# Three-branch attention of one layer: the compressed branch of two heads through one block-diagonal product

## The reference, cut to what matters

```python
k_cmp = compress(kvh(kc), pe_k, w1_k, w2_k)      # 31 compressed keys per key/value head
v_cmp = compress(kvh(vc), pe_v, w1_v, w2_v)
s = jnp.einsum('bsgrd,bngd->bgrsn', q, k_cmp).astype(jnp.float32) * scale
p, denom, _ = masked_softmax(s + bias_c, dist_c >= 0)
p_cmp = p / jnp.maximum(denom, 1e-30)
o_cmp = jnp.einsum('bgrsn,bngd->bsgrd', p_cmp, v_cmp.astype(jnp.float32))
...
o = g[..., 0:1] * o_cmp + g[..., 1:2] * o_sel + g[..., 2:3] * o_win
```

## Time and profile before

| what | us |
|---|---|
| median of the runs | 2892.97 |
| the profiled execution, its own time | 2896.67 |
| span of its trace, first to last instruction | 2894.5 |
| attention stage in it, first score product to the last drain | 1607.7 to 1761.5 |
| distance from one pair's drain to the next in the steady part | 18.56 |
| PE busy in the span | 2708.1 (94%) |
| DVE busy | 1883.1 (65%) |
| ACT busy | 843.7 (29%) |
| POOL busy | 1185.5 (41%) |

### The profile page before, as it was taken

One profiled execution on the slowest core, in us unless ns is written; L12 is line 12 of the kernel. 1 busy time (PEld: TensorE's weight loads), 2 busy tenths in 40 slices (PEclk: granted clock), 3 DMA queues, 4 the chain that ended last, 5 costly groups with the idle time before them and its releaser, 6 DMA issues.

```text
span 2894.5 us, 35802 instructions
## 1 busy us (share of the span) xinstructions
PE 2708.1 (94%) x12080; PEld 1729.9 (60%) x12080; DVE 1883.1 (65%) x4890; ACT 843.7 (29%) x1653; POOL 1185.5 (41%) x837
## 2 busy tenths in 40 slices
PE   8998999999877877799999999999999999999999
PEld 3364454444333332244447777888888877788887
DVE  8988788888888888777765786544223336554411
ACT  4732111111111111121123785322232127522222
POOL 5314444444444444344440233444434434444443
PEclk9999999999999999999999999999999999999999
DMA  4169999999999999999996221222322222122232
GB/s 131 62 238 372 417 412 421 421 418 420 412 421 419 414 422 414 421 421 420 420 420 229 64 69 53 96 99 94 107 87 99 93 67 67 66 95 95 102 101 79
DMA packets 130308, 700.38 MB, mean 242 GB/s; under 512 B 16694, under 2 KB 28886, under 8 KB 64343
## 3 DMA queue, kind: packets, MB, share of 16 engines
q0 software_dynamic: 74352, 543.04, 45.6%
q1 hardware_dynamic: 54760, 153.30, 15.7%
q10 hardware_dynamic: 1072, 2.41, 0.2%
HBM read 696.41 MB, written 2.28 MB: 241 GB/s over the span
## 4 chain that ended last, share of the span: by engine, by line
PE 49%; DMA 19%; issue 14%; DVE 8%; POOL 7%; ACT 3%; POOLq 0%; DVEq 0%; SPq 0%; ACTq 0%
DMA arena<-in_peer_uv,arena 18%; PE ps L543 16%; PE ps L883 14%; POOL w_lo L420 6%; PE ps L2363 4%; DVE arena L1216 3%; PE ps L911 2%; ACT arena L1662 1%; PE ps L2021 1%; PE ps L1570 1%; DVE arena L1227 1%; PE ps L795 1%; PE ps L1556 1%; PE ps L1542 1%; PE ps L773 1%
## 5 line engine op out<-in xcount | busy, mean ns | idle before, releaser
L883 PE MATMUL ps<-arena 128*128 128x512 f32 x2048 | 954.7, 610 | 145.6 <-DVE arena L1227 144.6
L1350 POOL DMA_INDIRECT arena<-in_peer_uv,arena x512 | 570.0, 1113 | 785.0 <-PE ps L883 723.4
L883 PEld LDWEIGHTS ps<-arena 128*128 128x128 f32 x2048 | 382.7, 193 | 653.7 <-issue 383.6
L1216 DVE CUSTOM_DVE_ANT_0 arena<-arena,sq 128x1024 f32<-128x1024 f32 x512 | 607.4, 1224 | 194.3 <-DMA arena<-in_peer_uv,arena 190.7
L420 POOL TENSOR_TENSOR w_lo<-ring,w_hi 128x1024 fp32r<-128x1024 f32 (+1 forms) x156 | 407.4, 2612 | 514.8 <-ACT w_hi L433 514.8
L543 PE MATMUL ps<-n_hi,w_hi 128*128 128x512 f32 x992 | 387.6, 391 | 0.5 <-issue 0.3
L543 PE MATMUL ps<-n_hi,w_lo 128*128 128x512 f32 x992 | 386.1, 389 | 0.0
L543 PE MATMUL ps<-n_lo,w_hi 128*128 128x512 f32 x992 | 382.0, 389 | 0.2 <-DVE n_lo L470 0.2
L1043 ACT ACTIVATE dots_gel<-dots_gel,tok_scale 128x2 f32<-128x2 f32 x256 | 75.7, 296 | 1002.2 <-DVE dots_gel L1216 1002.0
L433 ACT CAST w_hi<-ring 128x1024 fp32r<-128x1024 f32 (+1 forms) x156 | 174.6, 1120 | 644.3 <-PE ps L543 644.3
L543 PEld LDWEIGHTS ps<-n_hi,w_hi 128*128 128x128 f32 x992 | 186.2, 188 | 40.9 <-issue 2.4
(11 more groups left out here) (364 smaller groups left out, 3619.4 us busy)
## 6 DMA issues: line engine op xcount, KB each, us to landing
ring<-in_a_up SPq DMA_DIRECT2D x44, 512.0 KB, 3.5
ring<-in_b_up SPq DMA_DIRECT2D x44, 512.0 KB, 3.5
ring<-in_a_in SPq DMA_DIRECT2D x40, 512.0 KB, 7.7
ring<-in_b_q SPq DMA_DIRECT2D x24, 512.0 KB, 3.5
ring<-in_a_down SPq DMA_DIRECT2D x16, 704.0 KB, 4.0
ring<-in_b_down SPq DMA_DIRECT2D x16, 704.0 KB, 4.0
ring<-in_w_in SPq DMA_DIRECT2D x16, 512.0 KB, 3.5
arena<-in_peer_uv,arena POOLq DMA_INDIRECT x512, 10.9
```

The source lines that it names most:

```text
L883: mm = pe.matmul(bank(2 * (tt % 2) + q), diag[:, no % DIAGS, r, :], uvrow[p][r][:, D + 512 * q:D + 512 * q + 512], start=slot + r == 0, st ...
L1216: ins = dve.tensor_tensor_reduce(out=u, in0=u, in1=ntok[:, tt, :], scale=1.0, scalar=0.0, op0=ALU.mult, op1=ALU.add, accum_out=dots[:, p, ...
L1350: pool.indirect_dma_start(uvrow[p][r], None, t["peer_uv"], bass.IndirectOffsetOnAxis(ap=expert_id[:, tt, slot + r:slot + r + 1], axis=0)). ...
```

## The change

The compressed keys of the two halves are kept as a block-diagonal matrix (half 0 in rows 0 to 63 and columns 0 to 30, half 1 in rows 64 to 127 and columns 32 to 62, zeros elsewhere), and so are the compressed values (rows 0 to 30 with columns 0 to 63, rows 32 to 62 with columns 64 to 127). The scores of the compressed branch of both halves are then one product over all 128 rows with 63 columns, into bank 1 beside win 0; both blocks of probabilities are one transpose of 63 columns; and the output of both halves is one product over 63 rows with 128 output rows. Around it: the order of the products is sel 0, sel 1, cmp, win 0, win 1; DVE scales both compressed branches in one instruction and POOL only win 1; the last chunk of transposes is one block shorter; the row maxima of half 1 come as sel, cmp, win. ACT copies keys and values with four instructions instead of two, and DVE clears the padding.

```diff
-        kcmp = a.take(2, NCMP)
-        vcmp = a.take(256)
+        kcmp = a.take(2, 2, CMP_PAD)
+        vcmp = a.take(2, 2, DH)
...
+        def both_compressed(s):
+
+            it, qt = divmod(s, TT)
+            return (ps[:, 1, 384:384 + CMP_BOTH], proj[:, it, P * qt:P * qt + P],
+                    kcmp[:, it // GR].rearrange("p a b -> p (a b)")[:, 0:CMP_BOTH],
+                    vcmp[0:CMP_BOTH, it // GR].rearrange("p a b -> p (a b)"))
...
-        PE_ORDER = (("sel", 0), ("sel", 1), ("win", 0), ("win", 1), ("cmp", 0), ("cmp", 1))
-        DVE_ORDER = (("sel", 0), ("win", 0), ("cmp", 0), ("sel", 1), ("win", 1), ("cmp", 1))
-        READS_BEFORE = (1, 4, 3, 6, 3, 6)
-        SCORES_BEFORE = (1, 5, 5, 2, 6, 6)
+        PE_ORDER = (("sel", 0), ("sel", 1), ("cmp", None), ("win", 0), ("win", 1))
+        DVE_ORDER = (("sel", 0), ("win", 0), ("cmp", 0), ("sel", 1), ("cmp", 1), ("win", 1))
+        READS_BEFORE = (1, 4, 5, 5, 6)
+        SCORES_BEFORE = (1, 4, 4, 2, 4, 5)
...
-            return full + [(half, sides[half]["cmp"].blocks[0]) for half in range(2)], len(full)
+            return full + [(1, (Both.at, Both.width, both_compressed(s)[3]))], len(full)
...
-                    pe.matmul(b.scores, b.q, b.keys, start=True, stop=True).then_inc(LA.scores_ready, 1)
+                    if name == "cmp":
+                        to, q, keys, _ = both_compressed(s)
+                    else:
+                        b = branches(s, half)[name]
+                        to, q, keys = b.scores, b.q, b.keys
+                    pe.matmul(to, q, keys, start=True, stop=True).then_inc(LA.scores_ready, 1)
...
-                mm.then_inc(LA.pv_done, 1)
+                x, (_, width, v) = len(order) - 1, order[-1][1]
+                pe.matmul(ps[:, OUT_BANK, P * qt:P * qt + P], v, ptA[0:width, s % 2, P * x:P * x + P],
+                          start=False, stop=True).then_inc(LA.pv_done, 1)
...
-                for b in sides[0].values():
+                for b in (sides[0]["sel"], sides[0]["win"]):
...
-                dve.tensor_scalar(pr, pr, invA[:, s % 3, 1, 1:2], None, ALU.mult).then_inc(LA.scaled, 1)
-
+                dve.tensor_scalar(pr, pr, invA[:, s % 3, 1, 1:2], None, ALU.mult)
+                pr = pA[:, s % 3, Both.at:Both.at + 2 * CMP_PAD].rearrange("p (a b) -> p a b", a=2)[:, :, 0:NCMP]
+                dve.tensor_tensor(pr, pr, invA[:, s % 3, :, 0:1].broadcast_to([P, 2, NCMP]), ALU.mult).then_inc(LA.scaled, 1)
...
-                for b in (side["win"], side["cmp"]):
-                    pr = pA[:, s % 3, b.at:b.at + b.width]
-                    ins = pool.tensor_scalar(pr, pr, invA[:, s % 3, 1, b.slot:b.slot + 1], None, ALU.mult)
-                ins.then_inc(LA.scaled_rest, 1)
+                b = branches(s, 1)["win"]
+                pr = pA[:, s % 3, b.at:b.at + b.width]
+                pool.tensor_scalar(pr, pr, invA[:, s % 3, 1, b.slot:b.slot + 1], None, ALU.mult).then_inc(LA.scaled_rest, 1)
...
-            act.copy(kcmp, ps[:, 4, 0:62]).then_inc(cmp_copied, 1)
-            act.copy(vcmp[0:NCMP, :], ps[0:NCMP, 5, 0:256]).then_inc(cmp_copied, 1)
+            keep_keys()
+            keep_values()
...
+            dve.memset(kcmp, 0.0)
+            dve.memset(vcmp, 0.0)
```

More of the change, by code:

```diff
@@ L49 @@
 CMP_POS = 32
+CMP_PAD = 32
+CMP_BOTH = CMP_PAD + NCMP
 NEG = -1e30
@@ L1486, in branches @@
             wide = keys - P * k0
-            q, base = proj[rows, it, cols], 928 * half
+            q, base = proj[rows, it, cols], 896 * half
             return {
@@ L1492, in branches @@
                               tabA[:, it % 2, half, 896 - wide:896], 2, [vtok[:, 1, x, kv] for x in range(k0, qt + 1)]),
-                "cmp": Branch(half, 2 * half + 1, 384, NCMP, base + 896, q, kcmp[rows, gp, :],
-                              tcmp[:, heads(it)[half], 24 - 8 * qt:24 - 8 * qt + NCMP], 0, [vcmp[0:NCMP, kv]])}
-        PE_ORDER = (("sel", 0), ("sel", 1), ("win", 0), ("win", 1), ("cmp", 0), ("cmp", 1))
-        DVE_ORDER = (("sel", 0), ("win", 0), ("cmp", 0), ("sel", 1), ("win", 1), ("cmp", 1))
-        READS_BEFORE = (1, 4, 3, 6, 3, 6)
-        SCORES_BEFORE = (1, 5, 5, 2, 6, 6)
+                "cmp": Branch(half, 1, 384 + CMP_PAD * half, NCMP, 1792 + CMP_PAD * half, None, None,
+                              tcmp[:, heads(it)[half], 24 - 8 * qt:24 - 8 * qt + NCMP], 0, [None])}
+        def both_compressed(s):
[3 more added lines that the diff above has]
+                    vcmp[0:CMP_BOTH, it // GR].rearrange("p a b -> p (a b)"))
+        class Both:
+            at, width = 1792, CMP_BOTH
+        PE_ORDER = (("sel", 0), ("sel", 1), ("cmp", None), ("win", 0), ("win", 1))
+        DVE_ORDER = (("sel", 0), ("win", 0), ("cmp", 0), ("sel", 1), ("cmp", 1), ("win", 1))
+        READS_BEFORE = (1, 4, 5, 5, 6)
+        SCORES_BEFORE = (1, 4, 4, 2, 4, 5)
+        PER_SCORES = len(PE_ORDER)
         def turn_list(s):
@@ L1565, in values @@
                 order, _ = turn_list(s)
-                sides = [[(x, b) for x, (half, b) in enumerate(order) if half == side] for side in range(2)]
+                sides = [[(x, b) for x, (half, b) in enumerate(order[:-1]) if half == side] for side in range(2)]
                 for y in range(len(sides[0])):
@@ L1569, in values @@
                         x, (_, width, v) = sides[half][y]
-                        mm = pe.matmul(ps[64 * half:64 * half + 64, OUT_BANK, P * qt:P * qt + P], v,
-                                       ptA[0:width, s % 2, P * x:P * x + P], start=y == 0, stop=y == len(sides[0]) - 1)
-                mm.then_inc(LA.pv_done, 1)
+                        pe.matmul(ps[64 * half:64 * half + 64, OUT_BANK, P * qt:P * qt + P], v,
+                                  ptA[0:width, s % 2, P * x:P * x + P], start=y == 0, stop=False)
+                x, (_, width, v) = len(order) - 1, order[-1][1]
+                pe.matmul(ps[:, OUT_BANK, P * qt:P * qt + P], v, ptA[0:width, s % 2, P * x:P * x + P],
+                          start=False, stop=True).then_inc(LA.pv_done, 1)
             scores(0)
@@ L1609, in row_max @@
                     b = branches(s, half)[name]
-                    dve.wait_ge(LA.scores_ready, PER * s + SCORES_BEFORE[x])
+                    dve.wait_ge(LA.scores_ready, PER_SCORES * s + SCORES_BEFORE[x])
                     dve.tensor_tensor_reduce(
@@ L1641, in scale @@
                 pr = pA[:, s % 3, b.at:b.at + b.width]
-                dve.tensor_scalar(pr, pr, invA[:, s % 3, 1, 1:2], None, ALU.mult).then_inc(LA.scaled, 1)
+                dve.tensor_scalar(pr, pr, invA[:, s % 3, 1, 1:2], None, ALU.mult)
+                pr = pA[:, s % 3, Both.at:Both.at + 2 * CMP_PAD].rearrange("p (a b) -> p a b", a=2)[:, :, 0:NCMP]
+                dve.tensor_tensor(pr, pr, invA[:, s % 3, :, 0:1].broadcast_to([P, 2, NCMP]), ALU.mult).then_inc(LA.scaled, 1)
+            dve.wait_ge(hc_ready, 4)
+            for x in range(3):
+                dve.memset(pA[:, x, Both.at + NCMP:Both.at + CMP_PAD], 0.0)
             for s in range(STEPS + 2):
@@ L1659, in exponentials @@
                     act.wait_ge(LA.bank_read, PER * s + 3 * half + 3)
-                    for b in branches(s, half).values():
+                    for b in (branches(s, half)[x] for x in ("sel", "cmp", "win")):
                         pr = pA[:, s % 3, b.at:b.at + b.width]
@@ L2055, in layer_a_pe @@
                 u, half = divmod(g, 2)
+                rows = slice(CMP_PAD * half, CMP_PAD * half + NCMP)
                 for tile in range(2):
-                    mm = pe.matmul(ps[0:NCMP, 5, 64 * g:64 * g + 64], hg[:, 1, tile, half, NCMP * u:NCMP * u + NCMP],
+                    mm = pe.matmul(ps[rows, 5, 64 * g:64 * g + 64], hg[:, 1, tile, half, NCMP * u:NCMP * u + NCMP],
                                    w2[:, 1, tile, :], start=tile == 0, stop=tile == 1)
@@ L2069, in layer_a_act, with keep_keys, keep_values @@
         def layer_a_act(act):
+            def keep_keys():
+                for half in range(2):
+                    rows = slice(64 * half, 64 * half + 64)
+                    ins = act.copy(kcmp[rows, :, half, 0:NCMP], ps[rows, 4, 0:2 * NCMP].rearrange("p (a b) -> p a b", a=2))
+                ins.then_inc(cmp_copied, 1)
+            def keep_values():
+                for half in range(2):
+                    rows = slice(CMP_PAD * half, CMP_PAD * half + NCMP)
+                    ins = act.copy(vcmp[rows, :, half, :],
+                                   ps[rows, 5, 0:4 * DH].rearrange("p (a b c) -> p a b c", a=2, b=2)[:, :, half, :])
+                ins.then_inc(cmp_copied, 1)
             act.wait_ge(square_added, 2 * DK - 2)
```

2 lines of the change are left out of this document (removed).

## The result

The changed kernel takes 2903.22 us in the median of 7 runs (2899.92 to 2906.10), the kernel before 2891.67 (2890.69 to 2894.26). The ratio is 1.0038, with a 95% interval of 1.0028 to 1.0047: slower by 0.38%, or 11.0 us; the two medians are 11.55 us apart. Two later sets of 8 runs of the same changed kernel gave 1.0028 (1.0017 to 1.0039) and 1.0031 (1.0020 to 1.0042), medians 7.35 and 9.07 us above the kernel before, so 7 to 12 us is the fair statement. The direction is the forecast one; the forecast size was 5.8 us.

What follows compares the result with a forecast made beforehand. Bound: a chain of waits with an ACT leg and a PE leg, 18.56 us per pair. First pair 1.4, six periods 4.6, end -0.25, copies 0.1 sum to +5.8 us: 2898.8, range 2894.6 to 2903.2.

Steps and rivals of the forecast that it cites:

- The passes of the two halves were shared already: PE's compressed value products: both halves already share the array, so joining saves no pass; 0.42 against 0.37 us, +0.05.
- The additional score block, +0.44: PE's scores, per step: the 128-row product between sel and win costs 0.56 us against 0.14 for the pair, +0.44 with offsets.
- One sign that I had named: Trace after: weight loads should stop 0.2 us before the compressed product and again before win; loads running on would refute.
- Walking one pair, +0.76: Steady period between drains: PE's leg grows 0.76 us, the ACT leg's waits absorb as much; 18.56 becomes 19.32.
- just fits: First chunk of qt 1 in the ACT leg: its turn starts 0.38 us later, with 0.37 to 0.40 to spare.
- The ends, first pair +1.4: Start of the stage: DVE's second reading waits for win 0 behind the compressed product; +1.4 us, from 0.76 to 1.7.
- Four copies before the first score, +0.1: Ahead of the first score: four ACT copies instead of two cost +0.1 us (0 to 0.4).
- The end, -0.25: Last two steps, which have no scores: transposes, values and a shorter DVE copy together give -0.25 us.
- no cover: Rival, chance 0.12: PE's additional time in the ACT leg isn't absorbed; at full size 12 us, so 2904.7.

Runs made afterwards that it cites:

- e5_extra: Kernel before plus one unread product of 128 rows and 63 columns per score block, between sel and win: median 2904.26 us, ratio 1.0043.
- e2_two_scores: Changed kernel with compressed scores again two 64-row products in the old order and waits, values and transposes still joined: median 2891.77 us, ratio 1.0000.
- e3_cmp_first: Changed kernel with the one compressed score product moved to the front of the score block, behind the transposes: median 2894.11 us, ratio 1.0008.
- e4_first_full: Changed kernel with the compressed score product first and the compressed block of probabilities padded to 128 columns: median 2891.70 us, ratio 1.0001.
- the filled kernel: Changed kernel with three unused 256-column products of constants in PE's wait for ACT's copies before the first scores: pooled median 2898.66 us (22 runs).
- e1_warm: Changed kernel with three unused 256-column products of constants placed in PE's wait for ACT's copies, first set: median 2898.89 us (11 runs), ratio 1.0022.
- r3_warm: Changed kernel with PE's wait filled by the same three products of constants, repeated: median 2898.43 us (11 runs).
- e6_gap: Kernel before with four ACT copies instead of two ahead of the first score, nothing else: median 2892.81 us, ratio 1.0005.
- e7_all_warm: Changed kernel with compressed scores first, compressed block 128 wide and PE's wait filled with products of constants: median 2889.97 us, ratio 0.9994.

## Why the prediction was right and where it was too small

The direction was right. The range held the time only at its very edge: it ended at 2903.2 and the median is 2903.22. As a difference to the kernel before measured beside it, 11.55 us is more than the 10.2 at which the range ended, while the later sets, 7.35 and 9.07, lie inside. That the range reached so far is luck, since the term that takes the time there wasn't in the sum. Point by point:

- **The passes of the two halves were shared already.** Right. The joined value product takes 0.41 us against 0.37 (forecast 0.42), so nothing is saved there.
- **The additional score block, +0.44.** Right: 1.63 for 256 columns (forecast 1.64) and 2.06 for 384 (forecast 2.08). `e5_extra` shows 0.56 for a product of 63 columns in that place, `e2_two_scores` that nothing else lengthens the period. One sign that I had named came only by half: the loads stop ahead of the compressed product (0.33), but not for 0.2 us ahead of win. They run on in one row there, and the time shows only as the distance of 0.36 from the compressed product's first load to win's. Taken by the letter ("wrong if win follows the compressed product with loads running on") that sign would have spoken against a forecast whose cost was right. The Trainium skill's sentence that a change of tiling mode drains TensorE (TensorEngine Tiling (Array Packing), Tiling Modes) is borne out in both directions: removing such changes (`e3_cmp_first`, `e4_first_full`) gives time back. Its rule of about 60 cycles per matmul (Instruction Overhead) isn't, if it is read as a fixed cost of each record. By an estimate from that page, 25 ns for each of the three records that `e2_two_scores` saves per step, its period would be 18.29. It is 18.44, what 0.11 us per pass gives, with no more taken off.
- **Walking one pair, +0.76.** Right: +0.73. The sharpest point of it was that the first chunk of qt 1 "just fits". In the trace after, ACT goes from its exponentials into the two copies without a gap, 3.49 us after the drain as before, except in one pair. `e5_extra`, 0.56 per block, is past the point: its period grew by 0.24 more than its two blocks. The exception is the distance from the fifth drain to the sixth, 19.57, in all five traces of the changed and the filled kernel (19.57 or 19.58). It isn't this fit that fails there: PE starts that `turn` 2.73 us after the drain, as in the pair before (2.74), and ACT idles with no releaser that the profile names. The cause of these 0.28 us is open.

```profile
1718.24 1.07 ACT L1608 COPY arena<-ps 128x512 f32<-128x512 f32 x2 [0.17 <-issue]
```

- **The ends, first pair +1.4.** Too small, and the step that makes up the missing time. At full clock the start grew by 1.78 (`e1_warm`, `r3_warm`), near the 1.4 and just over the 1.7 that I gave as its upper end. What wasn't in it at all is the clock: 3.3 to 3.6 us where it falls. The walk took every duration of the start from rows at full clock and never asked whether a sparser start keeps it.
- **Four copies before the first score, +0.1.** The sum is right, by luck: PE's wait went from 0.76 to 1.26 us, 0.5 more, of which 0.42 came back because the compressed value products ahead of it, now in two column groups, take 0.66 us instead of 1.08. By themselves the four copies cost 0.39 (`e6_gap`), the upper end of what I gave them, and the faster products weren't in the prediction.
- **The end, -0.25.** -0.16 in the trace (16.27 against 16.43 from the seventh to the eighth drain).

Summed for the profiled executions: six periods 4.7 + start at full clock 1.8 - end 0.2 + copies 0.1 = 6.4 us, which is about what the filled kernel shows (2898.66 in 22 runs, 6.7 over the 2891.97 of all 94 runs of before; the filling itself puts the first score 0.17 us later), and some 3.5 for the clock, probably in most runs. None of the rivals in the prediction was this one; the time lies near where *no cover* would have put it, for another reason.

**What stays open.** What exactly makes the clock fall isn't settled. It fell in all three traces of the changed kernel and in the traces of `e2_two_scores` and `e4_first_full`, but not in that of `e3_cmp_first`, whose start is as sparse (PE busy 2.65 us of the four from 1606 to 1610, in 17 records, at a granted clock of 1.00), nor in that of `e6_gap`, whose wait is nearly as long. `e2_two_scores` has the long wait with the score blocks of before and fell; `e7_all_warm` has the wait filled with sparse blocks behind it and fell later. So the wait and the blocks behind it both seem to play a part, and chance; one trace per kernel can't tell how often. That filling the wait kept the clock up in the changed kernel's traces and narrows the spread of its runs is shown, and so is a lower median when the sets are pooled (within one call the gain of 0.7 to 2.4 us isn't clear of the noise); a rule is not.

## What to carry to other kernels

Count changes of array shape, not products: two half-array products of different halves run at once and cost one pass, while one full-array product between them cost 0.56 us here for 63 columns. If a product has to have another shape, put it next to work that has the same one (0.39 us less per step here), and pad it to that shape if need be (0.14 less). And where a change makes TensorE wait longer ahead of a stage, look at the granted clock behind the wait before adding up durations taken from full clock.

## What the runs showed that I had not expected

- The granted clock of TensorE stayed at 0.50 for 10.2 us (1607.9 to 1618.1) while PE was busy for 10.05 of them in the profile's count; busy time was no sign of work there, since only 27 records ran, against 56 in 10 us at full clock in `e1_warm`.
- Widening a value product from 63 rows to 128, with zeros, made it cheaper: 0.22 instead of 0.41 us up to the transposes, whose loads follow without the stop, and 0.14 in all.
- Writing the compressed values to two groups of output partitions took PE from 1.08 us to 0.66 (L2080 above) for the same 16 records. The row of before:

```profile
1605.88 1.08 PE L2057 MATMUL ps<-sq,arena 128*31 128x64 f32 x16
```
